# Summing the first tile's expert rows on VectorE, with earlier release of the gather ring and taps spread over 40 positions

## The reference, cut to what matters

```python
u = jnp.take(expert_u, e_flat, axis=0)
vv = jnp.take(expert_v, e_flat, axis=0)
act = jax.nn.gelu(jnp.einsum('td,tkd->tk', xb, u), approximate=False)
coef = (gate * act).astype(vv.dtype)
return jnp.einsum('tk,tkd->td', coef, vv)
```

## Time and profile before

| | |
|---|---|
| Median of 3 runs | 4052.86 us (4046.16 to 4052.99) |
| Profiled execution, its own time | 4054.08 us |
| Its span, first to last instruction | 4052.3 us |
| Mean granted TensorE clock | 0.850 |
| PE, DVE, ACT, POOL busy | 2865.7, 2703.9, 682.6, 1203.4 us |
| DMA moved | 1385.80 MB |

### The profile page before, as it was taken

The page is one execution under the profiler, slowest core; times in us unless marked ns, Lnnn a source line. Parts: engine busy times, 40 slices in busy tenths (PEclk is TensorE's granted clock), DMA queues, the critical chain, the costliest instruction groups (busy, mean ns, idle before and its releaser), DMA issues.

```text
span 4052.3 us, 41343 instructions
## 1 busy us (share of the span) xinstructions
PE 2865.7 (71%) x14768; PEld 1255.5 (31%) x14768; DVE 2703.9 (67%) x7412; ACT 682.6 (17%) x1484; POOL 1203.4 (30%) x1092
## 2 busy tenths in 40 slices
PE   6976554778567667666766876687677666779766
PEld 5422221334222313332332333233223332223311
DVE  4233343335586998699679868976997696445965
ACT  1200012210022013102310330132014101121000
POOL 0011111111144433433444344424333442223232
PEclk8987777889788888888888888879878988889989
DMA  9954468577689998998999899979988999999888
GB/s 334 345 202 155 151 225 290 206 277 291 226 328 408 411 366 326 422 413 345 372 419 400 330 395 419 394 290 416 414 355 325 421 408 391 415 417 365 335 329 349
DMA packets 217518, 1385.80 MB, mean 342 GB/s; under 512 B 27416, under 2 KB 38168, under 8 KB 66648
## 3 DMA queue, kind: packets, MB, share of 16 engines
q0 software_dynamic: 156672, 1140.92, 70.6%
q1 hardware_dynamic: 40384, 142.88, 9.8%
q10 hardware_dynamic: 20256, 99.35, 6.4%
HBM read 1369.94 MB, written 80.04 MB: 358 GB/s over the span
## 4 chain that ended last, share of the span: by engine, by line
PE 33%; DMA 29%; DVE 25%; issue 10%; POOL 2%; ACT 1%; DVEq 0%; ACTq 0%; POOLq 0%; SPq 0%
DMA t<-in_expert_uv,t 28%; PE psum L1367 20%; DVE t L1036 8%; PE psum L1214 4%; DVE t L1047 3%; PE psum L1256 2%; PE psum L1234 2%; POOL t L603 2%; DVE t L984 1%; DVE t L982 1%; DVE t L985 1%; DVE t L983 1%; PE psum L1245 1%; DVE t L927 1%; DVE t L981 1%
## 5 line engine op out<-in xcount | busy, mean ns | idle before, releaser
L1367 PE MATMUL psum<-t,t 64*64 64x512 f32 x5696 | 1627.2, 712 | 777.9 <-DVE t L1047 777.6
L603 POOL DMA_INDIRECT t<-in_expert_uv,t x1088 | 1203.2, 1106 | 2819.4 <-PE psum L1367 1403.2
L1036 DVE CUSTOM_DVE_ANT_0 t<-t,t 128x1024 f32<-128x1024 f32 x1088 | 1325.2, 1222 | 1039.0 <-DMA t<-in_expert_uv,t 1031.5
L1367 PEld LDWEIGHTS psum<-t,t 64*64 64x64 f32 x5696 | 415.9, 155 | 1746.1 <-DVE t L1047 983.1
L1363 PE MATMUL psum<-t,t 64*64 64x512 f32 x2496 | 760.4, 738 | 0.0
L754 ACT ACTIVATE t<-t 128x2 f32<-128x2 f32 x544 | 110.6, 203 | 2472.5 <-DVE t L1036 2465.6
L1047 DVE TENSOR_SCALAR t<-t,t,t 128x64 f32<-128x64 f32 x1088 | 294.0, 321 | 68.0 <-ACT t L754 59.1
L1324 PEld LDWEIGHTS psum<-t,t 128*128 128x128 f32 x2304 | 271.7, 197 | 54.0 <-issue 53.9
L1324 PE MATMUL psum<-t,t 128*128 128x128 f32 (+1 forms) x2304 | 281.8, 282 | 0.0
L1214 PE MATMUL psum<-t,t 128*128 128x128 f32 (+2 forms) x768 | 253.8, 489 | 8.2 <-DMA t<-in_xT 7.5
L903 DVE SCALAR_TENSOR_TENSOR t<-t,t,t 128x128 f32<-128x128 f32 x840 | 237.8, 344 | 0.0
(11 more groups left out here) (132 smaller groups left out, 1965.4 us busy)
## 6 DMA issues: line engine op xcount, KB each, us to landing
t<-in_wq_t ACTq DMA_DIRECT2D x63, 1024.0 KB
out<-in_cache_k_win SPq DMA_DIRECT2D x8, 4080.0 KB
out<-in_cache_v_win SPq DMA_DIRECT2D x8, 4080.0 KB
t<-in_w_in_t ACTq DMA_DIRECT2D x44, 512.0 KB, 5.1
t<-in_kc_t SPq DMA_DIRECT2D x8, 2560.0 KB
t<-in_vc_t SPq DMA_DIRECT2D x8, 2560.0 KB, 13.7
t<-in_expert_uv,t POOLq DMA_INDIRECT x1088
t<-in_w_v_t ACTq DMA_DIRECT2D x6, 1024.0 KB, 8.6
```

The source lines that it names most:

```text
L603: pool.indirect_dma_start(ring[:, r, :], None, I["expert_uv"], bass.IndirectOffsetOnAxis(ap=idn[t % 2][:, s:s + 1], axis=0)).then_inc(land ...
L1036: dve.tensor_tensor_reduce(out=ring[:, r, 0:D], in0=x1[t % 2][:, :], in1=ring[:, r, 0:D], scale=1.0, scalar=0.0, op0=ALU.mult, op1=ALU.add ...
L1367: last = pe.matmul(MAIN[t][half][NS * a:NS * a + NS, :], zt[NS * a:NS * a + NS, k % Z_RING, j, :], vv[NS * a:NS * a + NS, :], start=(p == ...
```

## The change

- **Tile 0's `v` rows are summed by DVE** (`first_values`). For each pair: one small product of gelu and gate (128x2), then for each slot one `scalar_tensor_tensor` over 128x1024 that multiplies the `v` row by the weight and adds it to `first_sum`, two PSUM banks, in place (the very first slot by `tensor_scalar`). PE has no product for tile 0. Each slot has its own event `v_done`, for which the gathers of tile 0 wait in place of `pv`.
- **Other tiles**: `weigh` is one small product (128x2) and one `tensor_tensor` over 128x128 that makes both diagonals, in place of two `tensor_scalar`. Pairs stay pairs.
- **The lags**: both lags are 1. On DVE the weighing at `q + 1` comes behind that position's dot, on PE the products come at `q + 1`. `zt` has 4 places. Tile 0's early slots are 48 in place of 49.
- **Taps**: the 31 taps are spread over 40 positions, and what needs them moves: convolution statistics from group 9 to 11, its output from 10 to 12, the output projection from groups 11 and 12 to group 13, the layer norm from 12 to 14 to 14 and 15, the transposes of `x1` to group 15, the queries from `i = 1` to `i = 3` of their group.
- Tiles 1 to 6 use the second pair of banks from pair 6 on in place of 8.

```diff
 RING, FIRST_RING = 9, 4
-Z_RING = 3
+Z_RING = 4
...
+TAP_SPAN = 40
...
-EARLY = ROUTE_STEP
-EARLY_GATES = (EARLY * (PH - 1) + TOP - 1) // TOP
+EARLY = 3 * TOP
+EARLY_GATES = EARLY // TOP
...
-AUX_PAIRS = range(8, PAIRS - 4)
+AUX_PAIRS = range(6, PAIRS - 4)
...
-        lo, hi = (min(max(q + j - ROUTE_AT - ROUTE_STEP, 0), early) for j in range(2))
+        lo, hi = (min(max(q + j - ROUTE_AT - ROUTE_STEP, 0), EARLY) for j in range(2))
     elif n == 0:
-        lo, hi = (early + (q + j) * (SLOTS - early) // SLOTS for j in range(2))
+        lo, hi = (EARLY + (q + j) * (SLOTS - EARLY) // SLOTS for j in range(2))
...
+def batches_at(n, q, lag):
+    return BATCH_PLACE.get(place(n, q) - lag, [])
+
+
+def tap_at(q):
+    return range(q * CK // TAP_SPAN, (q + 1) * CK // TAP_SPAN) if q < TAP_SPAN else range(0)
...
+        first_sum = psum[:, 6 * 512:8 * 512]
...
                     if s >= FIRST_RING:
-                        pool.wait_ge(pv, pair(0, s - FIRST_RING) + 1)
+                        pool.wait_ge(v_done, s - FIRST_RING + 1)
                 else:
                     k = (t - 1) * SLOTS + s
                     if k >= RING:
-                        pool.wait_ge(pv, pair(1, k - RING) + 1)
+                        pool.wait_ge(pv, (k - RING) // 2 + 1)
                     elif k < FIRST_RING:
-                        pool.wait_ge(pv, pair(0, SLOTS - FIRST_RING + k) + 1)
+                        pool.wait_ge(v_done, SLOTS - FIRST_RING + k + 1)
...
-            def gelu(t, p):
-                act.wait_ge(a_dot, SLOTS * t + 2 * p + 2)
-                d_ = dots[t % 2][:, 2 * p:2 * p + 2]
+            def gelu(t, c):
+                w = batch(t)
+                act.wait_ge(a_dot, SLOTS * t + w * (c + 1))
+                d_ = dots[t % 2][:, w * c:w * (c + 1)]
                 act.activation(d_, d_, ACT.Gelu).then_inc(a_gelu, 1)
...
+                for h in range(PH):
+                    if g == QUERY_AT[h] and i == 3:
+                        query_copy(m, h)
+                        if h == 0:
+                            x1_rows(m)
                 if i != 2:
                     return
-                if g == 9:
+                if g == 11:
                     conv_std(m)
-                if g == 10:
+                if g == 12:
                     conv_swish(m)
                     attended(m)
                     route_loads(m)
-                if g == 13:
+                if g == 14:
                     ln1_std(m)
-                if g == 14:
+                if g == 15:
                     x1_transposed(m)
                 for h in range(PH):
                     if g == QUERY_AT[h] + 1:
                         score_copy(m, h)
-                    if g == QUERY_AT[h]:
-                        query_copy(m, h)
-                        if h == 0:
-                            x1_rows(m)
 
...
-            def weigh(t, p):
-                k = PAIRS * t + p
-                dve.wait_ge(a_gelu, k + 1)
+            def weigh(t, c):
+                k = pair(t, c)
+                d2, g2 = dots[t % 2][:, 2 * c:2 * c + 2], gtn[t % 2][:, 2 * c:2 * c + 2]
+                dve.wait_ge(a_gelu, gelus(t, c) + 1)
+                step(dve.tensor_tensor(d2, d2, g2, ALU.mult))
                 if k >= Z_RING:
                     dve.wait_ge(pv, k - Z_RING + 1)
-                for j in range(2):
-                    s = 2 * p + j
-                    dve.tensor_scalar(zt[:, k % Z_RING, j, :], ident2[:, :], dots[t % 2][:, s:s + 1], gtn[t % 2][:, s:s + 1],
-                                      ALU.mult, ALU.mult).then_inc(zt_ready, 1)
+                dve.tensor_tensor(zt[:, k % Z_RING, :, :], ident2[:, :].unsqueeze(1).broadcast_to([P, 2, NS]),
+                                  d2.unsqueeze(2).broadcast_to([P, 2, NS]), ALU.mult).then_inc(zt_ready, 1)
+
+
+            def first_values(c):
+                d2 = dots[0][:, 2 * c:2 * c + 2]
+                dve.wait_ge(a_gelu, gelus(0, c) + 1)
+                step(dve.tensor_tensor(d2, d2, gtn[0][:, 2 * c:2 * c + 2], ALU.mult))
+                for s in (2 * c, 2 * c + 1):
+                    r, _ = spot(0, s)
+                    w_ = dots[0][:, s:s + 1]
+                    if s == 0:
+                        dve.tensor_scalar(first_sum, ring[:, r, D:ROW], w_, None, ALU.mult).then_inc(v_done, 1)
+                    else:
+                        dve.wait_ge(v_done, s)
+                        dve.scalar_tensor_tensor(first_sum, ring[:, r, D:ROW], w_, first_sum, ALU.mult, ALU.add).then_inc(v_done, 1)
 
             def residual(t):
                 r = rows(t)
-                if t in AUX_TILES:
+                if t == 0:
+                    dve.wait_ge(v_done, SLOTS)
+                elif t in AUX_TILES:
...
-                if m and 4 * g + i < CK:
-                    taps(m, 4 * g + i)
+                for k in tap_at(4 * g + i) if m else ():
+                    taps(m, k)
                 if i == 1 and 2 <= g < PH + 2:
                     weights_sum(m, g - 2)
                 if i == 2 and 1 <= g < PH + 1:
                     weights_max(m, g - 1)
-                if g == 9 and i == 2:
+                if g == 11 and i == 0:
                     conv_var(m)
-                if g == 9 and i == 3:
+                if g == 11 and i == 3:
                     conv_norm(m)
-                if g in (12, 13) and i == 2:
-                    ln1_half(m, g - 12)
-                if g == 14 and i == 0:
+                if g == 14 and i in (0, 1):
+                    ln1_half(m, i)
+                if g == 15 and i == 0:
                     ln1_end(m)
...
-                        for t, p in pairs_at(n, q, 2):
-                            weigh(t, p)
                         for s in slots_at(n, q):
                             dot(max(n, 0), s)
+                        for t, c in batches_at(n, q, 1):
+                            if t:
+                                weigh(t, c)
+                            else:
+                                first_values(c)
...
-                pe.wait_ge(zt_ready, 2 * (k + 1))
+                pe.wait_ge(zt_ready, k + 1)
...
-                if i != 1:
-                    return
-                if g == 8:
-                    conv_rows(m)
-                if g == 10:
-                    conv_back(m)
-                    att_transposes(m)
-                if g in (11, 12):
-                    out_projection(m, g - 11)
-                if g == 14:
-                    x1_transposes(m)
                 for h in range(PH):
-                    if g == QUERY_AT[h] + 1:
-                        key_scores(m, h)
-                    if g == QUERY_AT[h]:
+                    if g == QUERY_AT[h] and i == 3:
                         queries(m, h)
                         if h == 0:
                             x1_rows(m)
+                    if g == QUERY_AT[h] + 1 and i == 1:
+                        key_scores(m, h)
+                if g == 13 and i in (1, 3):
+                    out_projection(m, i // 2)
+                if i != 1:
+                    return
+                if g == 10:
+                    att_transposes(m)
+                    conv_rows(m)
+                if g == 12:
+                    conv_back(m)
+                if g == 15:
+                    x1_transposes(m)
 
             for n in range(-1, TILES + 1):
                 m = n + 1
                 for g in range(GROUPS):
                     for i in range(4):
-                        for t, p in pairs_at(n, 4 * g + i, 3):
-                            values_pair(t, p)
+                        for t, c in batches_at(n, 4 * g + i, 1):
+                            if t:
+                                values_pair(t, c)
                         if m < PT:
                             front(m, g, i)
                         elif m == PT:
```

More of the change, by code:

```diff
@@ L155, in place, with batch @@
     return SLOTS * (n + 1) + q
-PAIR_PLACE = {}
+def batch(t):
+    return 2
+BATCH_PLACE = {}
 for _n in range(-1, TILES):
@@ L162 @@
         for _s in slots_at(_n, _q):
-            if _s % 2:
-                PAIR_PLACE.setdefault(place(_n, _q), []).append((max(_n, 0), _s // 2))
-def pairs_at(n, q, lag):
-    return PAIR_PLACE.get(place(n, q) - lag, [])
+            _t = max(_n, 0)
+            if (_s + 1) % batch(_t) == 0:
+                BATCH_PLACE.setdefault(place(_n, _q), []).append((_t, _s // batch(_t)))
+def batches_at(n, q, lag):
+    return BATCH_PLACE.get(place(n, q) - lag, [])
+def tap_at(q):
+    return range(q * CK // TAP_SPAN, (q + 1) * CK // TAP_SPAN) if q < TAP_SPAN else range(0)
 def rows(n):
@@ L386, in build @@
         a_gelu = sem("a_gelu")
+        v_done = sem("v_done")
         zt_ready = sem("zt_ready")
@@ L434, in spot, with pair, gelus @@
             return k % RING, before + k // RING
-        def pair(t, s):
-            return PAIRS * t + s // 2
+        def pair(t, c):
+            return PAIRS * (t - 1) + c
+        def gelus(t, c):
```

(39 more changed lines are left out.)

3 lines of the change are left out of this document (1 added, 2 removed).

## The result

The changed kernel takes 3747.61 us, median of 4 runs (3743.52 to 3752.61), against 4052.93 for the kernel before: a ratio of 0.9251, interval 0.9235 to 0.9267. The forecast was 3770, range 3645 to 3890. The profiled execution has a span of 3745.3 us, 307 less than before.

The account below looks back on a forecast made before the run. Tile 0 was taken as bound by its loop through PE and a four-place ring, tiles 1 to 6 as near the transfer limit. 4054 - 124 - 79 - 72 - 8 = 3771, so 3770 us, range 3645 to 3890.

Parts of the forecast that it names:

- Tile 0 is a loop: Tile 0's slots: a chain of PE products, release, gather, landing, dot and weighing, about 13.1 us for two slots.
- Stage -1, -124: Tile 0's first 24 pairs: 10 us each, 240 us against 364, saving 124 us.
- The addition, 1.25 us: DVE's 1024-column addition from PSUM to PSUM in tile 0: 1.25 us, bounds 1.22 to 1.62.
- Stage 0, -79: Tile 0's next 40 pairs: 388 us of DMA time at share 0.83, so 467 us against 546, saving 79.
- the loops alone 340: Stage 0's 40 pairs: their loops by themselves put at 340 us, beside DVE load of 322 and DMA time of 388.
- Tiles 1 to 6, -72: Earlier release of ring places and a lighter tap stretch save 72 us, 12 a tile, bounds 30 and 130.
- I take half of the 145 us back: Tiles 1 to 6: half of 145 us of lost DMA time regained, since the taps don't touch some stretches.
- 0.9 us of slack a pair: Tiles 1 to 6: DVE busy 307 to 328 of 371 to 386 us, leaving about 0.9 us a pair.
- Tile 7, -8: Tile 7, 490 us at DMA share 0.92 with no taps: the shorter lag saves some 8 us.
- The moved front: Tile 0 before its first gather: same instructions in other groups, 0 us, bounds -4 and +4.
- rival C: Weighing nearer its gelu makes DVE wait, 2.3 us on each of 384 pairs in tiles 1 to 6: 4390 us; 3%.
- rival A: Tile 0's loop stays long through late landings, a 1.62 us addition and routing lumps: 3910 us; 15%.

Follow-up runs that it names:

- e5: The changed kernel with three ring places for tile 0 in place of four: 3919.79 us, ratio 0.9665.
- e6: The changed kernel with a second 1024-column addition, which frees nothing, behind each of tile 0's slots but the first: 3844.54 us, ratio 0.9482.
- e7: The changed kernel without the last 8 of the 16 cache blocks, which are not written: 3728.37 us, ratio 0.919.
- e8: The changed kernel with tile 0's additions of a pair ahead of the next pair's first dot: 3698.14 us, ratio 0.9125.
- e4: The changed kernel with the old lags for tiles 1 to 8 (weighing at q + 2, products at q + 3): 3768.23 us, ratio 0.9289.
- e1: The kernel before with only tile 0's part of the change (DVE additions, places freed by v_done): 3783.62 us, ratio 0.9331.
- e3: The changed kernel with the taps over 31 positions again in place of 40: 3756.51 us, ratio 0.9274.

## Why tiles 1 to 6 gained so little

The first three of these four start from the kernel with the additions first (ratio 0.9125). One measure of the noise: the change, e5, e6 and e7 differ in tile 0 alone, and their tiles 1 to 6 take 2230 to 2237 us. A few microseconds there tell nothing. The first dot, too, lies between 198 and 205 us through all these kernels.

**The closing layer norm's end three positions later.**

```diff
-                        if n >= 1 and q == RESIDUAL_AT + 5:
+                        if n >= 1 and q == RESIDUAL_AT + 8:
                             ln2_end(n - 1)
```

> The kernel with the additions first (e8, 3698 us), and the closing layer norm's end (reciprocal and three passes on DVE) three positions later, so that DVE no longer waits 4.9 us for ACT's square root in each tile's attention stretch. Theory D (DVE lags in that stretch): 3 to 5 us in each of tiles 1 to 7, about 3670. Theory P (PE's attention pieces hold the release of ring places): DVE's wait is hidden, within 8 us of 3698.

Measured: 3681.87 us, ratio 0.9074 (0.9059 to 0.9089), half a per cent or some 20 us faster. The wait of L1106 for ACT, in the base

```profile
DVE t L1106 <- ACT t L779: 22.0, 7, 5.0
```

is gone from the list. But its microseconds come back by half only: the wait for gelu grew from 123.2 to 133.9 us, and tiles 1 to 6 take 2216 us against 2228. Another 5 us of the profiled execution's gain lie before the first dot (198 against 202 us), which the edit doesn't touch. Theory D has the right direction, with 2 us a tile in place of 3 to 5, and nothing in tile 7.

**Weighing and products both at q + 2.**

```diff
-                        for s in slots_at(n, q):
-                            dot(max(n, 0), s)
-                        for t, c in batches_at(n, q, 1):
+                        for t, c in batches_at(n, q, 2):
                             if t:
                                 weigh(t, c)
+                        for s in slots_at(n, q):
+                            dot(max(n, 0), s)
...
-                        for t, c in batches_at(n, 4 * g + i, 1):
+                        for t, c in batches_at(n, 4 * g + i, 2):
```

> The kernel with the additions first (e8, 3698 us), with tiles 1 to 8 weighed at q + 2 ahead of that position's dot and multiplied on PE at q + 2. Against the lag of 1 a pair's gelu has one front more of time, and its ring places are freed a little later. Theory A (the wait for gelu, 126 us in all of after against 59 of before, costs): 10 to 25 us faster, about 3680. Theory P: the later release costs, up to 12 us slower; the lags of 2 and 3 cost 20 in e4.

Measured: 3649.3 us, ratio 0.8991 (0.8976 to 0.9006), 1.5% or about 50 us faster, twice what theory A gave it; theory P falls. The wait for gelu in the base, and here:

```profile
DVE t L1061 <- ACT t L770: 123.2, 73, 5.8
```

```profile
DVE t L1061 <- ACT t L770: 67.0, 72, 4.2
```

56 us of waiting went and tiles 1 to 6 take 2181 us in place of 2228. That isn't the gelu alone. In tiles 1 to 8, e4 differs from this kernel only in that PE's products stand at q + 3. Its wait for gelu is no larger (53 us), but its tiles 1 to 6 take 2247 us, 67 more (8 of them are what those tiles differ by between the change and e8). So one position of PE's products is worth at least as much as the wait for gelu, and of the three places that were tried, q + 1, q + 2 and q + 3, the middle one is the best. Tile 2 runs at a DMA share of 0.99 now:

```profile
1165.00:1521.00 356.00, 252.41 (x1488) 102.29 (x1486) 300.18 (x839) 71.56 (x159) 149.43 (x129) 0.86 0.99 403
```

**Eight ring places in place of nine for tiles 1 to 8.**

```diff
-RING, FIRST_RING = 9, 4
+RING, FIRST_RING = 8, 4
...
-        o_x = o_ring + RING * ROW * 4
+        o_x = o_ring + 9 * ROW * 4
```

> The kernel with the additions first (e8, 3698 us) and 8 ring places for tiles 1 to 8 in place of 9. Theory P (in tiles 1 to 7 the DMA runs dry only because ring places are not free in time in the attention stretch): one gather less in flight there costs about 2.5 us at each of several stalls a tile, 8 us a tile, 50 to 60 in all: 3750. Theory D (DVE's work in the stretch sets it, places are enough): under 15 us.

Measured: 3764.1 us, ratio 0.9265 (0.9241 to 0.9289), 1.5% slower, tiles 1 to 6 by 47 us and tile 7 by 10. Tile 2 falls back to a share of 0.96:

```profile
1184.00:1556.00 372.00, 261.63 (x1490) 106.86 (x1488) 300.93 (x840) 71.75 (x159) 150.67 (x128) 0.85 0.96 385
```

A place is worth 8 us a tile. So it is the time a slot occupies its place that counts in these tiles, and a wait of DVE for ACT lengthens it for every slot in the ring. That joins theories P and A: P names the scarce thing, A one of the waits that use it up. The last step of this is argued: no run lengthened a wait by itself.

**All of it together**: the last kernel but one (both at q + 2, ring of nine) with the layer norm's end at + 8.

```diff
-                        if n >= 1 and q == RESIDUAL_AT + 5:
+                        if n >= 1 and q == RESIDUAL_AT + 8:
                             ln2_end(n - 1)
```

> e10 (additions first, weighing and products both at q + 2; 3649 us) with the closing layer norm's end three positions later as in e9. Theory A+D (two waits of DVE for ACT in the same stretch, each with its own cost): the 16 us of e9 come off here too, about 3633. Rival P: with the wait for gelu gone the ring's places bind next, and the layer norm's 16 us shrink to under 5: 3645 or more.

Measured: 3635.47 us, 5 runs, ratio 0.8971 (0.8952 to 0.899). This beats both kernels: 10.3% under the kernel before and 3% under the changed one. Against e10 it is 0.2% in the ratio, with intervals that overlap (14 us in the plain medians, on different chips), so how much of the layer norm's gain is left is not settled by the times. In the two profiled executions tiles 1 to 6 take 2165 us against 2181, which is theory A+D's 16 us; and yet the wait of L1106 (23.8 us in e10) went while the wait for gelu grew from 67.0 us to

```profile
DVE t L1061 <- ACT t L770: 84.5, 75, 5.3
```

so the waits taken together shrank by only 6 us.

## Why the prediction was right, point by point

- **Tile 0 is a loop.** Right, and shown by e1 (the new release alone gives 265 us in tile 0), by e5 (taking one place away costs 178 us) and by e8 (44 us from the order alone).
- **Stage -1, -124.** Measured -131. The loop was put at 8.5 us plus 1.5 for lumps and contention and is 9.7. The landing takes 6.3 to 6.7 us in the rows above and 5.4 to 7.4 in the stretch's chain from 230 us on, mostly over the 5.6 that was assumed, and the lumps took less.
- **The addition, 1.25 us.** Measured 1.290, inside the bounds of 1.22 to 1.62. By the Trainium skill (page "VectorE: DVE Perf Modes", section on the TRN2 errata) a PSUM source with an SBUF target takes 120 + columns cycles, an estimate of 1.19 us here. The trace, with PSUM as the target too, is 0.10 over it.
- **Stage 0, -79.** Measured -130. This is the step that failed. I set its length by the DMA time, 388 us, over a share of 0.83 that a ring of four "won't" exceed. It reached 0.90, and e7 shows that the DMA wasn't the bound at all: without eight copies the stage is 20 us shorter, not 76. The term that stood beside it and was passed over was the right one, though it too was put too low: "the loops alone 340" is 40 loops of the bare 8.5 us. With the 10 us a pair that the same working used for stage -1 it would have been 400, near the 416 of the change and the 396 of e7.
- **Tiles 1 to 6, -72.** Measured -30. The two gains named (places freed earlier, lighter tap stretch) exist, at 15 to 20 us for the lag (e4) and under 10 for the taps (e3). Two steps failed. "I take half of the 145 us back" had no row behind it: by the same reckoning, length times (1.01 - share), 112 us are still lost in the new table. And the wait for gelu stood in a rival only, with nothing in the sum, since DVE was given 0.9 us of slack a pair and 1.4 us a pair were needed to undo the change. It came to 67 us more in all. e10 takes 56 us of it away and shortens these tiles by 47, but moves PE's products as well, so the wait's own price stays open. The slack was a mean over the tile, and the waits come in lumps of up to 5.8 us in its first half.
- **Tile 7, -8**, measured -14. **The moved front**, 0: the first dot of tile 0 is at 199.2 us, before 199.4.
- The errors in stage 0 (51 too little) and in tiles 1 to 6 (42 too much) nearly cancel. That the total came out within 22 us is luck in that part; the terms alone miss by twice that.
- Of the signs named beforehand: last dot of tile 0 at 840 us, not 905; DVE's share from 199 us on 0.78, not 0.7; tiles 1 to 6 at 365 to 378 us, not 355 to 370; the tap stretch of tile 2 at a share of 0.89 (1221 to 1332 us), not 0.95. Two signs of being wrong were there. The wait for gelu passed the 100 us that would speak for rival C; its mechanism was there, but 126 us are 0.33 us for each of the 384 pairs, where 1.4 were needed to undo the change. And the median time from issue to landing of stage -1's 48 gathers was 7.4 us, over the 7 that would speak for rival A; the loop was none the less 9.7 us, as the chain's own landings are shorter.

## What to carry to other kernels

Where a short ring feeds a chain of engines, write down the loop (release, transfer, each engine, release) and count the pairs. Length of the loop times number of pairs gives the stage as long as the loop binds, and an engine's or the DMA's share of 0.9 does not make it the bound. Then look at the order within one engine: here it paid to put an instruction that frees a place ahead of one that waits for a landing, and to let a consumer stand far enough behind another engine's result that it seldom waits, but no farther, since each position holds ring places. Don't take a mean share as slack for waits that come in lumps, and look at the parts of a stretch before calling a cause absent: what one part loses the next can give back (e3). Test by moving one position at a time; here that gave another 3% with no instruction less.

## What the runs showed that I had not expected

- An addition of 1024 columns with PSUM as source and target takes DVE 1.290 us, against 1.22 for the dot from SBUF to SBUF.
- A DMA share of 0.90 over 416 us left the stage nearly untouched when 33 MB of its transfers were removed (396 us at 0.74). The copies had filled gaps between gathers.
- With PE's products of tile 0 gone, TensorE's granted clock in the two stages read 0.73, after 0.79 and 0.83 with them. PE was busy 340 of 649 us there, and nothing waited for it in tile 0's loop, so it cost nothing that the runs show.
